# Attention gates of the prompt with their columns as the stationary operand, and merge gates dealt out by single products

## What is computed

```python
hq, hf, hi, hg, nq, kc, vc, ks, vs, kw, vw, ngate, mgate = jnp.split(h @ w_in, splits, axis=-1)
...
g = jax.nn.sigmoid(ngate.astype(jnp.float32)).reshape(B, L, 3, NSA_HEADS, 1)
o_nsa = g[:, :, 0] * o_cmp + g[:, :, 1] * o_slc + g[:, :, 2] * o_win
...
mg = jax.nn.sigmoid(mgate.astype(jnp.float32)).reshape(B, L, N_BRANCH, D_MODEL).astype(h.dtype)
merged = jnp.sum(mg * branches, axis=2)
```

## Time and profile before

| | us |
|---|---|
| median of 3 runs | 1179.52 (1179.44 to 1180.67) |
| the profiled execution | 1179.78 |
| its span, first to last instruction | 1178.0 |
| TensorE matmuls busy | 1148.1 (97%) |
| VectorE, ScalarE, GpSimd busy | 706.7 (60%), 544.7 (46%), 174.1 (15%) |
| mean granted TensorE clock | 0.99 of full speed |
| DMA | 143 GB/s over the span |

### The profile page before, as it was taken

The page is one execution under the profiler, slowest core; times in us unless marked ns, Lnnn a source line. Parts: engine busy times, 40 slices in busy tenths (PEclk is TensorE's granted clock), DMA queues, the critical chain, the costliest instruction groups (busy, mean ns, idle before and its releaser), DMA issues.

```text
span 1178.0 us, 21121 instructions
## 1 busy us (share of the span) xinstructions
PE 1148.1 (97%) x8613; PEld 1036.2 (88%) x8613; DVE 706.7 (60%) x1302; ACT 544.7 (46%) x867; POOL 174.1 (15%) x300
## 2 busy tenths in 40 slices
PE   6999999999999999999999999999999999999997
PEld 5987767678999999999999777667899999999997
DVE  5686255457567777763568633644756677777442
ACT  4532256464355555533454223664634555555232
POOL 1154300002120100100114441000311110010000
PEclk9999999999999999999999989999999999999998
DMA  9554422157644444334456525203784445432411
GB/s 289 163 148 164 155 73 72 42 167 209 237 143 144 143 144 145 124 127 158 144 126 208 170 73 177 72 1 110 198 275 148 143 157 160 158 131 90 145 59 45
DMA packets 151498, 165.99 MB, mean 141 GB/s; under 512 B 31492, under 2 KB 114214, under 8 KB 151078
## 3 DMA queue, kind: packets, MB, share of 16 engines
q1 hardware_dynamic: 151402, 164.64, 44.7%
HBM read 156.22 MB, written 12.46 MB: 143 GB/s over the span
## 4 chain that ended last, share of the span: by engine, by line
PE 91%; DVE 3%; POOL 1%; DMA 1%; ACT 1%; issue 1%; SPq 0%; DVEq 0%; POOLq 0%; ACTq 0%
PE mm L671 65%; PE ax L671 23%; PE ax L674 4%; DMA ring<-in_state_conv 1%; ACT mixb L1317 1%; DMA ring<-in_state_hgrn 1%; POOL rtmp L2315 0%; DVE ring_low L1674 0%; POOL rtmp L2312 0%; POOL work L2318 0%; DVE mixb L1824 0%; DVE mixb L2089 0%; ACT attb L1317 0%; POOL work L2317 0%; DVE work_parts L2058 0%
## 5 line engine op out<-in xcount | busy, mean ns | idle before, releaser
L671 PE MATMUL mm<-work_parts 128*128 128x320 f32 (+2 forms) x1120 | 356.4, 318 | 1.1 <-DVE h_low L1668 1.1
L1674 DVE TENSOR_TENSOR ring_low<-ring,work_parts 128x2048 fp32r<-128x2048 f32 (+2 forms) x116 | 256.0, 2207 | 125.4 <-ACT work_parts L1317 124.7
L671 PE MATMUL mm<-h_low,work_parts 128*128 128x320 f32 x1024 | 319.2, 312 | 0.0
L671 PE MATMUL mm<-work_parts,ring_low 128*128 128x320 f32 x1024 | 315.5, 308 | 0.0
L1317 ACT ACTIVATE work_parts<-ring 128x2048 fp32r<-128x2048 f32 (+2 forms) x116 | 211.9, 1826 | 159.6 <-PE mm L671 90.3
L671 PEld LDWEIGHTS mm<-work_parts 128*128 128x128 f32 (+1 forms) x1120 | 209.1, 187 | 9.2 <-issue 2.0
L671 PEld LDWEIGHTS mm<-h_low,work_parts 128*128 128x128 f32 x1024 | 192.9, 188 | 0.3
L671 PEld LDWEIGHTS mm<-work_parts,ring_low 128*128 128x128 f32 x1024 | 193.0, 188 | 0.0
L671 PE MATMUL ax<-act_parts,work_parts 128*128 128x320 f32 x544 | 126.1, 310 | 0.6 <-DVE ring L2080 0.6
L671 PE MATMUL mm<-act_parts,work_parts 128*128 128x320 f32 x480 | 117.4, 310 | 0.3 <-DVE merged_low L2058 0.3
L671 PE MATMUL mm<-hT,ring 128*128 128x320 f32 x384 | 111.9, 445 | 0.0
(11 more groups left out here) (235 smaller groups left out, 1593.6 us busy)
## 6 DMA issues: line engine op xcount, KB each, us to landing
ring<-in_w_gate_up SPq DMA_DIRECT2D x44, 1024.0 KB, 6.9
ring<-in_w_in SPq DMA_DIRECT2D x10, 2048.0 KB, 8.3
ring<-in_w_in SPq DMA_DIRECT2D x18, 1024.0 KB, 7.7
ring<-in_w_down SPq DMA_DIRECT2D x8, 1536.0 KB, 6.7
ring<-in_w_out SPq DMA_DIRECT2D x4, 2048.0 KB, 13.8
ring<-in_w_down SPq DMA_DIRECT2D x4, 2048.0 KB, 8.6
ring<-in_w_in SPq DMA_DIRECT2D x32, 128.0 KB, 3.1
ring<-in_cache_cmp_kv SPq DMA_DIRECT2D x32, 128.0 KB
```

The source lines that it names most:

```text
L671: return nc.tensor.matmul(out, lhsT, rhs, start=start, stop=stop)
L1674: V.tensor_tensor(unit_of(u, ring_r), unit_of(u, ring), unit_high(u).bitcast(F32), ALU.subtract).then_inc(*st.up(w_low[l]))
```

## The change

The prompt's gates leave `compressed_rows`. A new step `prompt_gates` (result `gtf`) takes 32 weight columns (24 gate columns and 8 others ahead of them) as the stationary operand and the 256 prompt tokens as the moving one, product k in the 32-partition strip k modulo 4 of one bank; each strip sums two of the eight products. ScalarE copies the bank to `gtF`. `prompt_gates_turned` (result `gtt`) multiplies `gtF` by `gsum`, a 0/1 matrix that VectorE builds once ahead of the first layer, which adds the four strips and turns the result to token rows; ScalarE's sigmoid of it fills `gts`. Both prompt tiles of the compressed rows now follow each other; the strips and the `nqr` products come next, and the keys are turned after those. VectorE and ScalarE empty in the new order. The merge-gate filling is dealt out by `merge_products`, in numbers of single products: 3, 7, 7, 7 for hb = 0 (before: 4, 4, 8, 8), and 8, 7, 7, 2 for hb = 1 (before: 8, 8, 8), the last two products behind the values of the second group. `mg0` and `kv0` change places in `BLOCKS`.

```diff
-BLOCKS = (["par", "w_hf", "w_hq", "w_nq", "cmp", "w_hi", "w_kvn", "w_kvc", "w_cmp", "w_hg", "kv0", "mg0", "mg1", "kv1",
+BLOCKS = (["par", "w_hf", "w_hq", "w_nq", "cmp", "w_hi", "w_kvn", "w_kvc", "w_cmp", "w_hg", "mg0", "kv0", "mg1", "kv1",
...
-                for k in range(KD if i < 2 else 0):
-                    last = mm(bank[0:TM[i], 256:280], hT[:, k, P * i:P * i + TM[i]], w[:, k, 256:280], k == 0,
-                              k == KD - 1)
                 last.then_inc(mm_full[L], 1)
...
+            def prompt_gates():
+
+                w = kt_of("w_kvc", KD, 280)
+                bank = begin(MM[L], "gtf")
+                for k in range(KD):
+                    strip = slice(32 * (k % 4), 32 * (k % 4) + 32)
+                    last = mm(bank[strip, 0:SEQ], w[:, k, 248:280], hT[:, k, 0:SEQ], k < 4, k >= 4)
+                last.then_inc(mm_full[L], 1)
+
+            def prompt_gates_turned():
+
+                bank = begin(AXR[L], "gtt")
+                pe.wait_ge(*MM[L].emptied_at("gtf"))
+                for i in range(2):
+                    last = mm(bank[:, 24 * i:24 * i + 24], gtF[:, P * i:P * i + P], gsum[:, :], True, True)
+                last.then_inc(ax_full[L], 1)
...
+            def merge_products(hb, at, n, l):
+
+                for g in range(3):
+                    first, end = max(at - KD * g, 0), min(at + n - KD * g, KD)
+                    if first < end:
+                        merge_gate(*GATES[hb][g], l, first, end)
...
                 compressed_rows(0, l)
+                compressed_rows(1, l)
+                prompt_gates()
+                for m in range(4):
+                    bank = begin(AXR[L], f"nqr{m}")
+                    pe.wait_ge(*MM[L].emptied_at(f"nq{m}"))
+                    mm(bank[:, 0:T], con("perm"), qraw[:, m, :], True, True).then_inc(ax_full[L], 1)
                 for x in range(2):
                     bank = begin(AXR[L], f"kt{x}")
...
-                compressed_rows(1, l)
-                for m in range(4):
-                    bank = begin(AXR[L], f"nqr{m}")
-                    pe.wait_ge(*MM[L].emptied_at(f"nq{m}"))
-                    mm(bank[:, 0:T], con("perm"), qraw[:, m, :], True, True).then_inc(ax_full[L], 1)
                 rows_turned(NSEQ)
                 compressed_rows(2, l)
+                prompt_gates_turned()
...
-                    merge_gate(*GATES[hb][0], l, None if hb else 1)
+                    merge_products(hb, 0 if hb else 3, 8 if hb else 7, l)
...
-                    merge_gate(*GATES[hb][1], l)
+                    merge_products(hb, 8 if hb else 10, 7, l)
...
-                    merge_gate(*GATES[hb][2], l)
+                    merge_products(hb, 15 if hb else 17, 7, l)
                     sample_values(n + 1, hb, 1)
                     if hb:
+                        merge_products(1, 22, 2, l)
                         sample_rows_turned(1)
...
-                        A(gts[:, i, :], bank[:, 256:280], ACT.Sigmoid)
                         A(ctok[:, i, :], bank[:, 0:256], ACT.Copy).then_inc(*st.up(mm_act[L]))
...
+                        bank = take(MM[L], "gtf")
+                        A(gtF, bank[:, 0:SEQ], ACT.Copy).then_inc(*st.up(mm_act[L]))
+                        bank = take(AXR[L], "kt0")
+                        A(ktn[:, 0, :], bank[:, 0:T], ACT.Copy).then_inc(*st.up(ax_act[L]))
...
+                bank = take(AXR[L], "gtt")
+                A(gts[:, 0:2, :], bank[:, 0:48].rearrange("p (i c) -> p i c", i=2), ACT.Sigmoid).then_inc(
+                    *st.up(ax_act[L]))
...
+            link(V.tensor_tensor(gsum[:, :], ident[:, 8:32], ident[:, 40:64], ALU.add))
+            link(V.tensor_tensor(gsum[:, :], gsum[:, :], ident[:, 72:96], ALU.add))
+            link(V.tensor_tensor(gsum[:, :], gsum[:, :], ident[:, 104:128], ALU.add))
```

More of the change, by code:

```diff
@@ L116, in mm_plan @@
     out = [("par", "V")] + [(f"hf{h}", "V") for h in range(HH)] + [(f"hq{h}", "V") for h in range(HH)]
-    out += [(f"nq{m}", "V") for m in range(4)] + [(f"{x}{i}", "A") for x in ("hi", "kvn", "kvc") for i in range(3)]
+    out += [(f"nq{m}", "V") for m in range(4)] + [(f"{x}{i}", "A") for x in ("hi", "kvn") for i in range(3)]
+    out += [("kvc0", "A"), ("kvc1", "A"), ("gtf", "A"), ("kvc2", "A")]
     out += [(f"hg{h}", "V") for h in range(HH)]
@@ L130, in ax_plan @@
     out += level_plan(3) + level_plan(4) + level_plan(5) + level_plan(6) + [(f"cc{s}", "A") for s in range(4, NSEQ)]
-    out += [("kt0", "A"), ("kt1", "V")] + [(f"nqr{m}", "V") for m in range(4)]
-    out += [("cp", "A"), ("hidk", "A"), ("hidv", "A"), ("gsel0", "V"), ("gsel1", "V")]
+    out += [(f"nqr{m}", "V") for m in range(4)] + [("kt0", "A"), ("kt1", "V")]
+    out += [("cp", "A"), ("gtt", "A"), ("hidk", "A"), ("hidv", "A"), ("gsel0", "V"), ("gsel1", "V")]
     out += [("kcm", "A")] + [(f"vc{n}", "A") for n in range(3)] + [("kcr", "V")]
@@ L267, in hybrid_step @@
         ctok = work[:, 6280:7048].rearrange("p (i c) -> p i c", i=3)
+        gtF = work[:, 7048:7048 + SEQ]
+        gsum = sb("gsum", 24)
         kvT = work[:, 7048:9096].rearrange("p (w b t) -> p w b t", w=2, b=4)
@@ L709, in compressed_rows, with feature_tile @@
                                       k == 0, k == KD - 1)
-                for k in range(KD if i < 2 else 0):
-                    last = mm(bank[0:TM[i], 256:280], hT[:, k, P * i:P * i + TM[i]], w[:, k, 256:280], k == 0,
-                              k == KD - 1)
                 last.then_inc(mm_full[L], 1)
-            def feature_tile(name, w, cols, half=None):
-                bank = MM[L].bank(name) if half == 1 else begin(MM[L], name)
-                for k in range(KD) if half is None else range(4 * half, 4 * half + 4):
+            def prompt_gates():
[11 more added lines that the diff above has]
+                last.then_inc(ax_full[L], 1)
+            def feature_tile(name, w, cols, first=0, end=KD):
+                bank = MM[L].bank(name) if first else begin(MM[L], name)
+                for k in range(first, end):
                     last = mm(bank[:, 0:T], cols(w, k), hT[:, k, :], k == 0, k == KD - 1)
-                if half != 0:
+                if end == KD:
                     last.then_inc(mm_full[L], 1)
@@ L911, in outputs_turned, with merge_gate @@
                     last.then_inc(ax_full[L], 1)
-            def merge_gate(m, y, l, half=None):
+            def merge_gate(m, y, l, first=0, end=KD):
                 mg = f"mg{m // 2}"
-                if m % 2 == 0 and y == 0:
+                if m % 2 == 0 and y == 0 and first == 0:
                     pe.wait_ge(*landed_at(mg, l))
                 w = kt_of(mg, KD, 512)
-                feature_tile(f"mg{'ab'[y]}{m}", w, plain(w, 256 * y + P * (m % 2)), half)
+                feature_tile(f"mg{'ab'[y]}{m}", w, plain(w, 256 * y + P * (m % 2)), first, end)
+            def merge_products(hb, at, n, l):
[3 more added lines that the diff above has]
+                        merge_gate(*GATES[hb][g], l, first, end)
             def level(kk):
@@ L1188, in layer @@
                     if hb == 0:
-                        merge_gate(*GATES[0][0], l, 0)
+                        merge_products(0, 0, 3, l)
                         turned(3)
@@ L1417, in layer @@
                         A(ctok[0:SMP, i, 0:140], bank[0:SMP, 0:140], ACT.Copy).then_inc(*st.up(mm_act[L]))
-                    if i == 0:
-                        bank = take(AXR[L], "kt0")
-                        A(ktn[:, 0, :], bank[:, 0:T], ACT.Copy).then_inc(*st.up(ax_act[L]))
                     if i == 1:
@@ L1938, in layer @@
                 ve.sem_inc(*st.up(ql_ready[L]))
-                bank = take(AXR[L], "kt1")
-                V.tensor_copy(ktn[:, 1, :], bank[:, 0:T]).then_inc(*st.up(ax_dve[L]))
                 for m in range(4):
@@ L1943, in layer @@
                     V.tensor_tensor(qT[:, m, :], bank[:, 0:T], con("sinq"), ALU.mult).then_inc(*st.up(ax_dve[L]))
+                bank = take(AXR[L], "kt1")
+                V.tensor_copy(ktn[:, 1, :], bank[:, 0:T]).then_inc(*st.up(ax_dve[L]))
                 for m in range(4):
```

## The result

The changed kernel took 1172.45 us (median of 6 runs, 1169.5 to 1175.13), the one before 1180.28 beside it (6 runs): a ratio of 0.9931, 95% interval 0.9910 to 0.9953. It is 8 us faster, where 16 were forecast, and 1172.45 lies outside the range of 1158.5 to 1169. The profiled execution is the fastest of the six, 1169.5 us with a span of 1167.7.

The account below looks back on a forecast made before the run. TensorE's own queue, busy 97% of the span, was taken as the bound. Terms -14.9 - 2.7 - 0.9 + 0.3 + 2.4 = -15.8 us gave 1163.7 us on the median, range 1158.5 to 1169.

Parts of the forecast that it names:

- The clock elsewhere: Half-clock stretches outside the compressed rows, 1.7 us each, taken as unchanged, with bounds of -3.4 and +3.4 us.
- the first part: Compressed rows of both layers with gate strips and later keys: 6.85 and 8.03 us less, -14.9 together.
- The state load: Sample attention's end: st1, issued later, lands after 6.0 us; TensorE waits 1.5 us a layer, net +2.4.
- the slower rival: st1 shares queues with br0 and lands with it; 10.1 us wait a layer plus half clock: 1184.3, chance 0.03.
- The compressed rows: First prompt tile to hidden layer: 14.0 us a layer at full clock, from 20.85 and 22.03.
- the 64-token tile, the strips' copy, `cp` and the turning product: Terms of the compressed rows' sum, per layer: 1.96 us, nothing, 0.53 and 0.47.
- GpSimd's keys: Compressed rows: rotated keys ready 8.16 us after the first prompt tile begins, reached at 10.2, so no wait.
- Changes of array shape: Sample attention: one more filling stretch a layer, two more shape changes at 0.15 together, +0.3 us for both layers.
- The sample attention's waits: Waits for scaled probabilities (-2.7 us) and for VectorE's rows ahead of ovt1 (-0.9), both layers, would go.
- the strips': Rival: strips in the compressed rows run one after the other, 2.5 x 2 more: 1168.7, chance 0.06.
- the keys': Rival: the key wait in the compressed rows only moves, 2.85 us a layer and half clock stay: 1174.5, chance 0.03.
- The half clock's rival: Half clock still granted in the compressed rows though the wait is gone: +5.1 us, 1168.8, chance 0.09.

Follow-up runs that it names:

- e12: The kernel before, with six thrown-away products ahead of the first prompt tile of either layer, in front of TensorE's wait for rotated keys: 1176.74 us, ratio 0.9976.
- e9: The changed kernel with sample outputs reordered, heads 0 and 1 of both sequence halves first, so the second state load is wanted later: 1166.20 us, ratio 0.9889.
- e1: The changed kernel itself, run again without any edit for a second profile and more times: 1172.97 us.
- e4: The changed kernel with 8, 8, 8 merge products in the sample attention's second half, none behind its values: 1168.13 us, ratio 0.9877.
- e6: The changed kernel with four of the second output gate's eight 320-column products moved into the middle of the compressed scores: 1171.35 us.
- e11: The changed kernel with kv0 ahead of mg0 in the order of loads, as before the change: 1172.59 us.
- e5: The changed kernel with four thrown-away products ahead of layer 1's compressed rows, so all that follows comes 1.8 us later: 1173.02 us.
- e2: The kernel before with only the gate strips and later keys; merge products and load order as before: 1169.11 us, ratio 0.9897.

## Why the prediction was wrong

- **The clock elsewhere, "I take them as unchanged": this is the step that failed.** Of the 14.9 us of the first part, 5.1 were half-clock time. They went at their place, and e12 shows that the idle time had caused them. But the loss of a whole run didn't fall by 5.1: it was 12.9 us in the mean of the 52 runs of before (11.8 in the median), and 13.1 and 14.8 in the two sets of the changed kernel (13.5 and 15.2). The half clock came back at the compressed scores of layer 2, behind the state wait and, in some executions, near the end. This is 5 to 7 of the 8 us by which the gain fell short of 15.8. Its bounds of 3.4 either way were made from two stretches of one profile; places that stood at 1.00 in it were not counted.
- **The state load: mechanism right, size wrong.** The wait came where it was put. It was 3.5 us more than before in the first profile, 2.8 in the second, not 2.4: I took 6.0 us for the landing, where layer 2 had shown 7.1 and took 7.1 again. Its other price, the half clock behind it, 3.4 us in the first profile, was given to the slower rival alone, for a wait of 10 us. It came behind all three waits of 2.1 to 2.7 us, and behind some of 1.4 and 1.8. e9 has neither the long wait nor that stretch, and is 6.3 to 6.8 us faster, about 3 of them at full clock.
- **The compressed rows** came to 14.55 instead of 14.0 a layer. The key transposes cost 1.08 (forecast 0.8, from `cp`, whose four records are all of 128 rows; two of these six are of 64, so changes of shape stand among them); the 64-token tile, the strips' copy, `cp` and the turning product were within 0.1 of their terms. The strips ran beside each other; GpSimd's keys were in time.
- **Changes of array shape** were put too low, 0.08 us each. From one start to the next a group holds one change, the one behind it, and the prediction's 4.40 / 16 held one as well. Sixteen records of state products go from 813.22 to 813.79 in e9, 0.57 us, and 32 took 1.01: a change is 2 x 0.57 - 1.01 = 0.13. Merge products ahead of the same scores show more. These are 14 records of the changed kernel, in 3.97 us, and the start of the scores behind them:

```profile
203.29 4.04 PE L674 MATMUL mm<-hT,ring 128*128 128x320 f32 x14
207.26 1.83 PE L674 MATMUL ax<-work 64*32 64x256 f32 x28
```

  Before, eight took 2.35, so a record is 0.27 and the change 0.19. Ahead of the values it is some 0.08 (14 records in 3.87, 209.84 to 213.71). The rule of the Trainium skill, page "TensorEngine Tiling (Array Packing)", section "Key Properties", that a change of tiling mode drains the engine was weighed in the prediction with 0.16 a change and 1 us in all; that estimate lies within the 0.08 to 0.19 of these rows.
- **The sample attention's waits** of 2.7 and 0.9 went as forecast. The seven products took 3.97 us (203.29 to 207.26), beside 3.85.
- **Not in the prediction:** a wait of 0.3 us ahead of the copies of the convolution rows, which every kernel with the keys turned later shows, and 0.6 us by which the first load came later in the profiled execution.
- **The rivals:** the strips' and the keys' were wrong, the slower one too. The keys' time, 1174.5, was the nearest to 1172.45, by luck, since the keys were in time. The half clock's rival had the right size, 5.1 us that aren't saved, but at the wrong place: the compressed rows were at 1.00.
- At full clock the whole forecast was -15.8 + 5.1 = -10.7; measured are -7.9 and -8.7. The terms above make up the difference: 1.1 for the compressed rows, 0.4 to 1.1 for the state load, 0.3 for the new wait and 0.2 to 0.5 for the four changes of shape.

What stays open is what decides which of the thin places is at half clock in an execution. One program differs from run to run (e1, e4), two waits of the same length at the same place have 0.50 and 1.00 behind them (e6, e11), and whether a shift of 1.8 us moves the stretches (e5) is not shown.

## What to carry to other kernels

Time at half clock that a change removes is no sure gain: book work and waits at full clock, and put the whole of the clock's share into the range, with its source in several executions of the kernel rather than one profile. Where a change shortens the time between a load's release and its use, take the longest landing that the trace shows there, and add what a wait can draw behind it. Sending the release off ahead of the filling work (e4), or moving the first use back by independent work (e9), was worth 3 to 4 us here at full clock, against the 8 to 9 of the change itself.

## What the runs showed of the hardware

- TensorE was granted 1.2 GHz over 10 us in which it was busy without a gap (e2, 1149.10 to 1159.10; e4, 1148.10 to 1158.00). What it did just ahead, here in e4 (start, length, instruction), was 3 us of one-column products:

```profile
1144.47 3.02 PE L674 MATMUL ax<-consts,mixb 128*128 128x1 f32 x24
1147.36 0.54 PE L674 MATMUL ax<-act_parts,work_parts 128*128 128x320 f32 x2
1147.73 0.31 PE L674 MATMUL ax<-act_parts,ring_low 128*128 128x320 f32 x1
```

  In e4's stretch itself 320-column products take some 5.4 us from start to start, and more one-column products and transposes, from 1150.19 to 1153.70 and from 1157.04 on, the other 4.5. So a gap in TensorE's work isn't needed for the lower level; narrow products stood ahead of it here, at the compressed scores and at the hidden layer. They don't always draw it: in the first profile of the changed kernel the same products and what follows them are at 1.00 (1148.00 to 1158.00).
- Filling a wait with products whose results are thrown away made a kernel 2.9 us faster (e12).
- Four strips of 128 rows by 32 columns with 256 columns moving ran beside each other: 16 records in 1.0 us, a full tile's 16 in 3.5.
